# Page numbers of a decoder step: eight side by side in one register load, in place of eight checked loads

## The reference, cut to what matters

```python
def gather_pages(pool, page_table):
    rows = pool[page_table]
    return rows.reshape((page_table.shape[0], -1) + pool.shape[2:])

def diff_sample(qb, kb, vb, cache_k, cache_v, page_table, bias_b, lam, lam_init, subln_g):
    ...
    k_all = jnp.concatenate([gather_pages(cache_k, page_table).astype(kb.dtype), kb], axis=1)
    v_all = jnp.concatenate([gather_pages(cache_v, page_table).astype(vb.dtype), vb], axis=1)
    return diff_core(qb, k_all, v_all, past + jnp.arange(t), jnp.arange(past + t), bias_b, lam, lam_init, subln_g)
```

## Time and profile before

| | |
|---|---|
| median of 3 runs | 2515.99 us (2514.65 to 2521.67) |
| the profiled execution, its own time | 2510.16 us |
| its span in the profile | 2508.3 us |
| mean granted TensorE clock | 0.969 of full speed |
| PE busy | 2276.0 us, 91% |
| PE weight loads | 1521.5 us, 61% |
| DVE / ACT / POOL busy | 44% / 30% / 17% |
| DMA, mean over the span | 112 GB/s |
| DMA, 700 to 800 us | 326 GB/s, engines 0.96 busy |

### The profile page before, as it was taken

How to read it: one execution, slowest core, us unless ns; L and a number is a source line. 1 busy time by engine, 2 the same in 40 slices (tenths; PEclk the granted TensorE clock), 3 DMA queues, 4 the chain that set the end, 5 groups by cost and what they waited for, 6 DMA issues and landing times. The chain is left out here.

```text
span 2508.3 us, 34326 instructions
## 1 busy us (share of the span) xinstructions
PE 2276.0 (91%) x12165; PEld 1521.5 (61%) x12185; DVE 1104.2 (44%) x2683; ACT 764.6 (30%) x2065; POOL 419.5 (17%) x447
## 2 busy tenths in 40 slices
PE   7999997767888888888799898989999999999999
PEld 5644443444555555545444346468888888888887
DVE  5479998753455533343313113344333433370001
ACT  3552245653555454444301015211111111100000
POOL 1352123111000000133100010023121312102110
PEclk9999998998999999999799999999999999999999
DMA  4211101005999799955240203211111111122221
GB/s 144 73 64 69 43 9 68 1 1 195 316 325 323 249 318 306 321 194 196 98 153 1 84 24 145 78 43 35 47 39 42 44 37 49 35 79 70 72 65 40
DMA packets 184496, 281.88 MB, mean 112 GB/s; under 512 B 17590, under 2 KB 86886, under 8 KB 184326
## 3 DMA queue, kind: packets, MB, share of 16 engines
q1 hardware_dynamic: 154518, 224.75, 27.0%
q0 software_dynamic: 11520, 41.95, 4.7%
q10 hardware_dynamic: 18288, 12.98, 1.7%
HBM read 261.69 MB, written 17.94 MB: 111 GB/s over the span
## 5 line engine op out<-in xcount | busy, mean ns | idle before, releaser
L635 PE MATMUL PS<-region 128*128 128x512 f32 (+5 forms) x864 | 327.7, 534 | 1.3 <-DVE region L470 1.3
L2804 PE MATMUL PS<-region,ffn_w 128*128 128x264 f32 x1408 | 323.5, 389 | 1.6 <-PEq L2254 1.6
L2804 PEld LDWEIGHTS PS<-region,ffn_w 128*128 128x128 f32 x1408 | 269.5, 191 | 48.6 <-issue 2.0
L2024 ACT COPY region<-PS 128x512 f32<-128x512 f32 x352 | 194.2, 592 | 190.7 <-PE PS L1896 97.4
L635 PEld LDWEIGHTS PS<-region 128*128 128x128 f32 (+1 forms) x864 | 152.7, 181 | 160.7 <-issue 140.4
L2804 PE MATMUL PS<-region,side 128*128 128x264 f32 x1056 | 243.3, 387 | 1.4 <-POOL side L2761 1.4
L2804 PEld LDWEIGHTS PS<-region,side 128*128 128x128 f32 x1056 | 198.9, 190 | 34.9 <-POOL side L2761 1.5
L1896 PE MATMUL PS<-ident_f,region 128*128 128x128 f32 x1024 | 147.5, 289 | 42.2 <-DMA region<-cache_b_k 21.4
L932 DVE TENSOR_SCALAR_CACHE_REDUCE mask<-score,cand 128x384 bf16<-128x384 f32 (+2 forms) x198 | 180.9, 942 | 3.4
L1896 PEld LDWEIGHTS PS<-ident_f,region 128*128 128x128 f32 x1024 | 117.5, 147 | 71.3 <-DMA region<-cache_b_k 36.2
L1110 POOL DMA_INDIRECT region<-cache_a_k,gather_a x22 | 21.4, 973 | 483.8 <-PE PS L1896 462.8
(11 more groups left out here) (443 smaller groups left out, 3811.1 us busy)
## 6 DMA issues: line engine op xcount, KB each, us to landing
region<-cache_b_k SPq DMA_DIRECT2D x256, 256.0 KB, 3.7
region<-cache_b_v SPq DMA_DIRECT2D x128, 256.0 KB, 4.9
sa_more_values<-cache_b_v SPq DMA_DIRECT2D x64, 256.0 KB
side<-cache_b_v SPq DMA_DIRECT2D x64, 256.0 KB
ffn_w<-w_gate SPq DMA_DIRECT2D x11, 1024.0 KB, 5.3
ffn_w<-w_up SPq DMA_DIRECT2D x11, 1024.0 KB, 5.4
region<-w_in SPq DMA_DIRECT2D x4, 2048.0 KB, 7.8
ffn_w<-w_down ACTq DMA_DIRECT2D x7, 704.0 KB, 5.5
```

Of the source, the lines that this page charges most:

```text
L635: last = nc.tensor.matmul(M.PS[0:n, s % 3, 0:chunks[j].width], XT[:, c, t * P:t * P + n], w[j % 2][:, c, 0:chunks[j].width], start=(c == 0 ...
L2024: nc.scalar.copy(dst, M.PS[0:dst.shape[0], T0 + x % 2, 0:dst.shape[1]]).then_inc(t_read, 1)
L2804: last = nc.tensor.matmul(M.PS[:, bank, 0:TW], left[:, c, :], right[:, c, :], start=begin and c == 0, stop=(c == KH - 1), skip_group_check ...
```

## The change

`M.pages` keeps its size, but is laid out anew: the eight page numbers that a unit needs lie side by side in one partition. Unit u finds them in partition u // 4, columns 8 (u % 4) to 8 (u % 4) + 7, in the order j, i. To bring them there, eight DMAs, one for each sequence, take the place of the one of L289: each reads the 32 numbers of a sequence and writes 16 runs of two numbers (8 bytes) into four partitions. At the top of each unit one call loads eight registers of SP from that partition, with no check of bounds at run time; the `value_load` inside the loop is gone. The DMAs of keys and values, their waits and their order stay.

```diff
@@ Setup.other_loads
-        sp.dma_start(M.pages[:], io["page_table"][:]).then_inc(M.pages_loaded, 16)
+        for b in range(DEC_B):
+            g, j = divmod(b, 4)
+            sp.dma_start(M.pages[4 * g:4 * g + 4, :].rearrange("q (c j i) -> q c j i", j=4, i=RKB)[:, :, j, :],
+                         io["page_table"][b].rearrange("(q c i) -> q c i", q=4, i=RKB)).then_inc(M.pages_loaded, 16)
@@ sample_attention, sync
-        eng.wait_ge(M.pages_loaded, 16)
+        eng.wait_ge(M.pages_loaded, 16 * DEC_B)
         for u in range(walk.first_a):
             kind, g, c = chunks[walk.units[u]]
-            page = {}
+            q, x = divmod(u, 4)
+            _, page = nc.values_load_multi_w_load_instructions(
+                M.pages[q:q + 1, 8 * x:8 * x + 8], engines=[mybir.EngineType.SP], min_val=0, max_val=n_pool - 1,
+                skip_runtime_bounds_check_because="the page table holds rows of the pool")
             for v in range(2):
                 for j in range(4):
-                    b = 4 * g + j
...
                     for i in range(2):
-                        if v == 0:
-                            page[j, i] = eng.value_load(M.pages[b:b + 1, 2 * c + i:2 * c + i + 1], min_val=0,
-                                                        max_val=n_pool - 1)
                         eng.dma_start(out[:, i * 512:(i + 1) * 512],
-                                      pages_b[v][bass.ds(page[j, i], 1)].rearrange("o s f -> (o s) f")
+                                      pages_b[v][bass.ds(page[2 * j + i], 1)].rearrange("o s f -> (o s) f")
                                       ).then_inc(arrived, 16)
```

## The result

| | kernel before | changed kernel |
|---|---|---|
| median of the first comparison | 2515.65 us (4 runs, 2514.65 to 2521.67) | 2487.36 us (4 runs, 2486.39 to 2496.06) |
| ratio, 95% interval | | 0.9899 [0.988, 0.9918] |
| the same kernels again, another comparison | 2511.3 us (9 runs) | 2489.65 us (5 runs), 0.9913 [0.99, 0.9927] |
| profiled execution | 2510.16 us | 2487.41 us |

The changed kernel is faster by 22 to 28 us, about 1%.

A forecast was written before the change was run, and what follows sets the result against it. PE, 91% busy, was taken as the bound, idling where SP's loads came late. Gaps -10.7, clock -0.6 and start +0.3 made -11.0 us, from the median 2515.99 to 2505.0 us; range 2492 to 2517.

The forecast's parts named there:

- the gaps that PE would lose: In the B units, half of PE's 21.4 us of waits for keys would go: 10.7 us, between 6.9 and 21.4.
- the clock: In the B units, fewer long PE gaps mean fewer falls of the granted clock: 0.6 us gained, nothing at the lower end.
- PE, with its order of two streams, needs almost the same 12.9 us per unit as SP.: In the B units, PE would follow a faster SP only until its own chain with ACT and DVE holds it.
- Its gaps are 13.2 us on 90.8 us of work, 0.145: PE's gap share at 726 to 830 us, applied to two other stretches: 3.3 and 3.6 us less, 6.9 us gained.
- The fear that ACT's copies would take over the waits for keys: At the line turning keys, PE would meet its partners sooner and wait for them; ACT's copies already cost 17.5 us.
- the upper bound, 2.4 us: Most the clock could give in the B units: 0.03 x 81.5 us, if all the lost clock were regained.
- SP's unit from 12.9 to 9.1 us (8.2 to 10.1): SP's time per B unit: 5.0 us of single loads and checks go, 1.2 us for one load of eight comes.
- 1.2 us for the load of eight: Cost on SP, once per B unit, of loading eight registers, taken between 0.27 and 2.2 us.
- The DMAs can follow: In the B units, DMA engines could move a unit's 4.19 MB in 11.7 us at 360 GB/s, or 12.4 at 339.
- +0.3 us for the start: At the program's start, eight page loads ahead of `w_in` delay PE's first projection matmul: 0.3 us, from nothing to 2.5.
- What would show it: Signs: key waits under 3 us, SP's waits up 118 us or more, over 340 GB/s, stage end 8 to 15 us earlier.
- Rival (a): In the B units every PE wait for keys goes and the lost clock returns: -23.5 us, 2492.5 us; chance 0.13.

## Why the prediction was wrong in size

The direction and the mechanism were right: SP was late, its loads were the reason, and the transfers could follow. The sum failed in two terms: the gaps that PE would lose, 10.7 us where 16.1 to 17.6 were measured, and the clock, 0.6 us where 9.0 to 9.7 were.

**"PE, with its order of two streams, needs almost the same 12.9 us per unit as SP."** This is the reading that failed first. PE *took* 12.9 us because two engines that hand buffers to each other show the same period in any trace, whichever of them sets it. PE's own need was 11.5 us in units 2 to 9, as the changed kernel shows, and with loads added to SP it rose to 12.8, 13.6 and 15.6. SP, with waits of 32 us in all 32 units, had the period of its own work, and that already said which of the two was led.

**"Its gaps are 13.2 us on 90.8 us of work, 0.145", carried over to the other stretches.** The stretch 726 to 830 us was taken as PE's way without late keys, and 6.9 us followed as the lower end, towards which the 10.7 was drawn. But its gaps belong to its own units. In the changed kernel units 9 to 16 and 20 to 28 are:

```profile
725.60:827.50 101.90, 87.92 (x815) 55.26 (x818) 63.28 (x197) 53.11 (x146) 0.00 (x0) 0.98 0.89 308
880.70:979.20 98.50, 89.61 (x903) 58.24 (x904) 37.99 (x110) 55.45 (x132) 0.00 (x0) 1.00 0.98 349
```

The first still has 14.0 us of gaps on 87.9 us, 0.16. The second has 8.9 on 89.6, 0.10, and units 2 to 9 have 8.1 on 72.5, 0.11. What holds PE in units 9 to 16 are waits that belong to them, by PE's waits in the changed kernel from 725.6 to 827.5 us:

```profile
PE PS L1898 <- ACT region L2026: 5.1, 10, 1.6
PE PS L1875 <- DVE sa_mask L2080: 2.7, 4, 1.8
PE PS L1959 <- ACT region L2026: 2.0, 4, 1.0
PE PS L1959 <- ACT sa_prob L2036: 1.6, 1, 1.6
PE PS L1980 <- ACT sa_pt L2026: 1.3, 1, 1.3
```

The kernel before has the same list in these units, within 0.4 us a line, and 1.4 us for keys. Units 20 to 28 have no wait for DVE's mask or for `sa_prob` in either. A list of waits by partner would have shown that the comparison stretch was another kind of stretch. The fear that ACT's copies would take over the waits for keys was put at half of 21.4 us; the waits for ACT at that line grew by about 3 us, and 16 to 18 us were gained.

**"I take 0.6 us", for the clock.** It was 9 us. The mean clock of one stretch, 0.94, was set against 0.97 of the comparison stretch, and for 81.5 us only. In the changed kernel PE has 1.00 in units 2 to 9 and 72.5 us of work where there were 77.8 (the two rows above). The four profiles there with SP's unit at 13.0 or 13.1 us have 76.4 to 80.7 us at 0.91 to 0.96, and four with 11.7 us or less 72.5 to 72.7 us at 1.00. Over the whole B part it is 370.4 for 379.4. With late keys put back it returns: 388.4 us busy at 0.94 with eight more loads, 403.0 at 0.92 with twelve, for the same matmuls. So the upper bound, 2.4 us, was no bound. One set of gaps costs twice: as itself, and in the work behind it, as the earlier trace rows had shown in one place. (The runs show that late keys, a lower granted clock and longer busy time go together, and come and go with SP's loads; which single gaps lower the clock was not traced beyond rows 8.)

The other steps, one by one:

- *SP's unit from 12.9 to 9.1 us (8.2 to 10.1).* 13.0 to 9.2 us. That it fits so well is luck: a checked load costs 0.53 to 0.57 us, not the 0.63 by which a key page exceeded a value page, and the load of eight 0.53 us, not 1.2, and the two errors cancel.
- *1.2 us for the load of eight.* 0.53 us. The Trainium skill (DMA: Bandwidth & Descriptors, "Latency and other measured facts") gives about 600 ns as the floor of one such load; here eight registers took less than that. As said, the price is no term of the sum.
- *The DMAs can follow.* Right: 376 GB/s in units 2 to 9, where the kernel before has 324 at nearly the same share.
- *+0.3 us for the start.* Right in effect. The page loads took 5.92 us, beyond the estimate of 3.8, but the layout with them measured 1.0006 in ratio. PE's first projection matmul comes at 23.96 to 24.81 us in the five profiles without the eight loads ahead of `w_in` and at 24.17 to 25.13 in the eleven with them, 0.3 us later in the mean.
- *What would show it.* The waits for keys gone, ACT's waits slightly up, over 340 GB/s: as written. Eight key pages took 3.95 us in unit 2 and up to 5.8 us in the next seven, where SP waits between them. SP's waits for PE grew from 31.9 to 129.3 us (95.5 and 33.8), by 97 and not by 118 or more, since PE's unit became shorter too. The first matmul of the profile, at 24.78 us, lay just past the 24 to 24.6 given. The end of the part came 23.5 us earlier (1044.7 to 1021.2), not 8 to 15.

Rival (a), PE follows in full, said -23.5 us, and it was -22.75 between the profiles, though by other pieces: less of the waits (17.6 of 21.4) and more of the clock (9.7 for 2.4), against a later beginning; that its sum came so near is in part luck. It had a chance of 0.13, and the stretch 726 to 830 us was the one argument against it. The forecast was written from a median of three runs, 2515.99, which lay above those of the later comparisons (2510.1 to 2514.4); this put it 2 to 6 us higher still.

What stays open: why the B part begins 1.9 us later on average. The kernel with the old layout and unchecked single loads has it too (601.1 us), in one profile, which speaks against both the page loads and the load of eight as its cause. No version beat the changed kernel: the one with late page loads has 0.9905 [0.9888, 0.9922] against its 0.9899 and 0.9913.

## What to carry to other kernels

Two engines that share buffers show one period. Before taking it for both, add up each one's own work and its waits: the one that hardly waits leads, and the other's own pace is hidden. Take a comparison stretch only from units that wait for the same partners, and price late data twice, as the gap and as the slower work of PE behind it. An added cost meant as an experiment must be found in the trace before its time is read, since unused work may not be in the program.

## What the runs showed of the hardware

- One instruction on SP that loads eight registers from neighbouring places took 0.53 us, one that loads a single register 0.27 us: 37 ns for each of the seven more, if they cost the same. A checked load cost SP 0.53 to 0.57 us with all around it.
- The eight small page loads took SP 5.92 us, 0.74 us each, beside 0.43 us for each of the six loads just ahead of them. The loads of `w_in` behind them were issued 4.2 us later (17.54 for 13.32) and landed 6.5 to 7.8 us after their issue, where they had taken 7.6 to 10.7, so that most of the delay did not reach PE.
- The share of the DMA engines' time was 0.96 at 324 GB/s and 1.03 at 376 for the same units: a share near 1 was not a limit reached.
- PE's busy time for the same work ran from 368.6 us (granted clock 0.97) to 403.0 us (0.92), in kernels that differ in SP's register loads alone.
